# The adaLN modulation of a two-layer streaming encoder, in blocks of 512 features turned by VectorE, sixteen of them between stages

## The reference

```python
c_act = jax.nn.silu(c)
mods = (c_act @ w_ada[l] + b_ada[l]).reshape(bsz, N_SUB, 3, D_MODEL)
shift, scale, gate = mods[:, :, 0], mods[:, :, 1], 1 + mods[:, :, 2]
h = _modulate(x, shift[:, 0], scale[:, 0])            # x * (1 + scale) + shift
f1 = _swiglu(h, ffn_w_gate[l, 0], ffn_w_up[l, 0], ffn_w_down[l, 0])
x = _layer_norm(ALPHA * x + 0.5 * gate[:, 0, None, :] * f1, ln_g[l, 0], ln_b[l, 0])
```

## Time and profile before

| what | value |
|---|---|
| median of 3 runs | 1809.65 us (1809.06 to 1810.31) |
| the profiled execution | 1802.38 us, its span 1800.6 us |
| TensorE (PE) busy | 1669.1 us (93%) |
| VectorE (DVE) busy | 760.9 us (42%) |
| ScalarE (ACT) busy | 648.4 us (36%) |
| GpSimd (POOL) busy | 255.9 us (14%) |
| bytes moved | 301.42 MB, 167 GB/s over the span |
| mean granted TensorE clock | 0.969 |

### The profile page before, as it was taken

One profiled execution on the slowest core, in us unless ns is written; L12 is line 12 of the kernel. 1 busy time (PEld: TensorE's weight loads), 2 busy tenths in 40 slices (PEclk: granted clock), 3 DMA queues, 4 the chain that ended last, 5 costly groups with the idle time before them and its releaser, 6 DMA issues. The chain is left out here.

```text
span 1800.6 us, 30095 instructions
## 1 busy us (share of the span) xinstructions
PE 1669.1 (93%) x11414; PEld 1520.8 (84%) x11414; DVE 760.9 (42%) x1042; ACT 648.4 (36%) x1114; POOL 255.9 (14%) x286
## 2 busy tenths in 40 slices
PE   5999999789977999999789999999889997999996
PEld 3999999678757999989688999989776586999996
DVE  2433333532258433343652433344534465343454
ACT  3433333332244433333342433333334334333332
POOL 1200011220126000011250000011230143000021
PEclk9999999989978999999899999999899998999998
DMA  7544465559813353556335453556353742434441
GB/s 284 211 171 178 160 222 187 201 164 270 253 37 105 142 208 140 198 189 221 120 86 187 168 194 143 206 188 215 112 194 103 271 162 93 141 123 134 129 141 47
DMA packets 88240, 301.42 MB, mean 167 GB/s; under 512 B 11048, under 2 KB 15816, under 8 KB 86736
## 3 DMA queue, kind: packets, MB, share of 16 engines
q1 hardware_dynamic: 83072, 287.62, 46.3%
q10 hardware_dynamic: 5088, 12.69, 2.4%
HBM read 283.58 MB, written 6.00 MB: 161 GB/s over the span
## 5 line engine op out<-in xcount | busy, mean ns | idle before, releaser
L1242 PE MATMUL bank<-hH,wH 128*128 128x384 f32 x1536 | 525.7, 342 | 14.9 <-DVE hL L986 14.1
L623 ACT ACTIVATE wH<-raw 128x1024 fp32r<-128x1024 f32 x328 | 345.1, 1058 | 523.1 <-PE bank L1242 416.7
L903 DVE TENSOR_TENSOR wL<-raw,wH 128x1024 fp32r<-128x1024 f32 x328 | 414.6, 1289 | 251.8 <-ACT wH L623 249.2
L1242 PE MATMUL bank<-hL,wH 128*128 128x384 f32 x1536 | 517.0, 337 | 0.0
L1242 PE MATMUL bank<-hH,wL 128*128 128x384 f32 x1536 | 516.8, 336 | 0.0
L1242 PEld LDWEIGHTS bank<-hH,wH 128*128 128x128 f32 x1536 | 291.0, 189 | 31.3 <-issue 23.4
L1242 PEld LDWEIGHTS bank<-hL,wH 128*128 128x128 f32 x1536 | 291.1, 190 | 0.4
L1242 PEld LDWEIGHTS bank<-hH,wL 128*128 128x128 f32 x1536 | 290.7, 189 | 0.0
L1033 DVE TENSOR_TENSOR tmp<-sg,bank 128x384 f32<-128x384 f32 x88 | 48.7, 554 | 479.1 <-PE bank L1242 451.7
L1242 PE MATMUL bank<-hidH,wH 128*128 128x384 f32 x704 | 241.3, 343 | 0.0
L1242 PE MATMUL bank<-hidL,wH 128*128 128x384 f32 x704 | 235.6, 335 | 0.0
(11 more groups left out here) (169 smaller groups left out, 1628.2 us busy)
## 6 DMA issues: line engine op xcount, KB each, us to landing
raw<-W SPq DMA_DIRECT2D x328, 512.0 KB, 6.0
araw<-ADA SPq DMA_DIRECT2D x130, 512.0 KB, 4.3
land<-ADA SPq DMA_DIRECT2D x16, 512.0 KB, 15.1
KTb<-kt_d SPq DMA_DIRECT2D x8, 1024.0 KB, 6.1
Vb<-v_d SPq DMA_DIRECT2D x8, 1024.0 KB, 5.2
araw<-ADA ACTq DMA_DIRECT2D x14, 512.0 KB, 6.2
u<-uF SPq DMA_DIRECT2D x64, 81.5 KB, 4.9
u<-uF ACTq DMA_DIRECT2D x64, 81.5 KB, 5.2
```

Source lines behind the costliest of these rows:

```text
L623: a.activation(wH[:, slot, :], raw[:, slot, :], ACT.Copy).then_inc(w_hi, 1)
L903: v.tensor_tensor(wL[:, slot, :], raw[:, slot, :], wH[:, slot, :].bitcast(F32), ALU.subtract)\
L1242: op = mm(out, tile_w(w, slot, k), m[:, k0 + k, :], start=start and k == 0 and q == 0, stop=stop and k == nk - 1 and q == 2)
```

## The change

The eight first chunks stay chunks of 256 features with 32 short matmuls each (64 columns). The other 72 become 36 blocks of 512 features. A block is four pieces of 512 KB (`ADA` laid out anew), each two of the eight input feature tiles. TensorE makes a piece with 8 matmuls of 128 columns, and the four column groups now hold other output features instead of other input features, so nothing is left to be added. VectorE turns a block with one transpose of 32 x 32 squares and adds the bias (`modulation`). `ada_tr`, `adaS` and ScalarE's two instructions are gone.

The table `PLACES` gives each piece its tile. By it 16 blocks stand between stages, behind `stats` on TensorE (`gap_block`): 3 after FFN0, 2 after the convolution, 3 after pw2, 3 after FFN1, 3 after FFN2, 2 after O. Their pieces go to tiles that lie over memory free at that time (`gapH` and `gapL` over `hH` and `hL`, `gapD` and `gapE` over the hidden layer). The other 20 use the two halves of `araw` as before: 5 in the gate/up loop of FFN0 and of FFN1, 3 in that of FFN2 (each over two steps, a piece in each half step), 1 and 2 in the down products of FFN0 and FFN1, 1 in the convolution, 3 in the attention, none in FFN3.

Besides, `u4` has three slots, the taps of a tile are loaded behind its shifted rows, the `wf` matmuls stand behind the K stage's `lead`, and VectorE splits four units of K before it waits for them.

```diff
+PLACES = (6 * [RAW4] + [GAP_A, GAP_B, GAP_E] + [RAW4] + [GAP_A, GAP_B] + [GAP_D, GAP_F, GAP_E]
+          + 7 * [RAW4] + [GAP_A, GAP_B, GAP_E] + 3 * [RAW4] + [GAP_A, GAP_B, GAP_E] + 3 * [RAW4] + [GAP_D, GAP_F])
...
-        FFN_ADA = [(8, 11, 8), (35, 11, 8), (54, 11, 8), (77, 3, 0)]
+        FFN_ADA = [(0, 5, 1), (15, 5, 2), (25, 3, 0), (36, 0, 0)]
+        FFN_GAP = [(6, 7, 8), (22, 23, 24), (28, 29, 30), ()]
...
@@ SyncE
-            def ada_chunk(c):
-                sp.wait_ge(a_mm, c)
-                for j in range(2):
-                    sp.dma_start(araw[:, j], ADA[2 * c + j]).then_inc(a_in[j], 16)
+            def loop_piece(s, kq):
+                sp.wait_ge(a_mm, 4 * s + kq + 1)
+                sp.dma_start(araw[:, kq % 2], ADA[4 * s + kq]).then_inc(piece_in[RAW4[kq]], 16)
...
-                with sp.Fori(0, na) as i:
-                    ada_chunk(c + i)
-                    w_units(u + RING + RING * i, RING)
+                if n_up:
+                    with sp.Fori(0, n_up) as i:
+                        for half in range(2):
+                            loop_piece(s + i, 2 * half)
+                            loop_piece(s + i, 2 * half + 1)
+                            w_units(u + RING + 8 * i + 4 * half, RING)
+                with sp.Fori(2 * n_up, 11) as i:
                     w_units(u + RING + RING * i, RING)
...
+                    w_unit(u + 48 + m, m % RING)
+                sp.wait_ge(w_used, u + FFN_UNITS)
+                for kq in range(4):
+                    piece(gap[2], kq)
...
@@ VectorE
+            def modulation(s, bank=ADB):
+                dve.wait_ge(a_mm, 4 * s + 6)
+                dve.wait_ge(a_mod, s + 1)
+                v.transpose(adaT[:].rearrange("p m c -> p (m c)"), bank[:, 0:P]).then_inc(a_tv, 1)
+                dve.wait_ge(a_tv, s + 2)
+                k = 2 * FIRST_CHUNKS + 4 * s
+                v.tensor_tensor(mods[:, bass.ds(k, 4), :], adaT[:, :, 0:NG],
+                                pcol("b_ada", k, 4).unsqueeze(2).to_broadcast([P, 4, NG]), ALU.add).then_inc(a_mod, 1)
...
+            dve.sem_inc(a_mm, 2)
+            dve.sem_inc(a_tv, 1)
+            dve.sem_inc(a_mod, 1)
...
@@ TensorE
+            def four_blocks(out, cols, tile, k, start, stop):
+                for j in range(4):
+                    op = mm(out[32 * j:32 * j + 32, 0:cols], cact[:, k, :], tile[:, cols * j:cols * j + cols],
+                            start=start, stop=stop)
+                return op
+            def ada_piece(kq, tile, bank=ADB):
+                for kk in range(2):
+                    op = four_blocks(bank, P, tile[:, kk], 2 * kq + kk, kq + kk == 0, kq + kk == 4)
                 op.then_inc(a_mm, 1)
...
+            def gap_block(s, place, second=bank[5]):
+                out = second if place == 1 else ADB
+                pe.wait_ge(a_tv, s + 1 if place == 0 else s)
...
-                with pe.Fori(1, na) as i:
-                    gate_up(i, True, c + i - 1)
+                if n_up:
+                    with pe.Fori(0, n_up) as i:
+                        gate_up(2 * i + 1, s + i, 0)
+                        gate_up(2 * i + 2, s + i, 1)
```

More of the change, by code:

```diff
@@ L321, in w_units, with piece @@
                     w_unit(n + j, j % RING, wait)
-            def ada_chunk(c):
-                sp.wait_ge(a_mm, c)
-                for j in range(2):
-                    sp.dma_start(araw[:, j], ADA[2 * c + j]).then_inc(a_in[j], 16)
+            def piece(s, kq):
+                place, before = PLACES[s][kq], PIECE_USES[4 * s + kq][1]
+                if before is not None and place[:3] == "raw":
+                    sp.wait_ge(a_mm, eaten(before))
+                sp.dma_start(piece_tile(place), ADA[4 * s + kq]).then_inc(piece_in[place], 16)
@@ L939, in normalise @@
                 if h:
+                    if gap:
+                        dve.wait_ge(a_mm, last_in("HL", gap) if any(PLACES[s][1][0] in "HL" for s in gap) else 2)
                     rest(*h, 0, 1)
                     rest(*h, 1, 1)
+                if gap:
+                    modulation(gap[0])
+                    modulation(gap[1], second)
                 mean_out(4, 2)
@@ L1149, in _ @@
             modulate(4)
-            for n in range(U_K + RING, U_V + RING):
+            for n in range(U_V, U_V + RING):
                 refill(n, n % RING)
@@ L1204, in body @@
                 for j in range(4):
+                    if kind == "p" and j == 1 and (not isinstance(i, int) or i > 0):
+                        modulation(B_ATT - 1 + i)
                     if scores:
@@ L1307, in stats, with gate_up @@
                 mm(VAR[:, 0:T], ones, sqb[:, 1], start=False, stop=True).then_inc(var_ok, 1)
+                for place, s in enumerate(gap):
+                    gap_block(s, place, second)
             def ffn(fi):
-                u, (c, na, nd) = FFN_U[fi], FFN_ADA[fi]
+                u, (s, n_up, n_down) = FFN_U[fi], FFN_ADA[fi]
                 m = FFN_M[fi]
-                def gate_up(i, with_ada, turn_of=None):
+                def gate_up(i, block=None, half=0):
                     for j in range(2):
@@ L1527, in turn, with body @@
                 nc.tensor.transpose(bank[4 + (j + 1) % 2][:, 384:512], om[:, j % 2, :], ident).then_inc(o_mm, 1)
[L1529 removed]
+            def body(kind, i, block=None, new=True):
                 for j in range(4):
@@ L1539, in body @@
                         turn(*jo)
-                    if with_ada and j == 2:
-                        ada_mm(CH_S4 + i, araw, ring_waits(CH_S4 + i))
-                    if with_ada and j == 3:
-                        ada_tr(CH_S4 + i)
-            body("p", 0, True)
-            with pe.Fori(1, 4) as i:
-                body("p", i, True)
+                    if block is not None:
+                        loop_piece(block, B_ATT, j)
+            body("p", 0, B_ATT)
+            with pe.Fori(1, 3) as i:
+                body("p", i, B_ATT + i)
+            body("p", 3)
             body("s", 0)
```

384 lines of the change are left out of this document (216 added, 168 removed).

## The result

The changed kernel takes **1988.68 us** (median of 4 runs, 1983.57 to 1991.97), the kernel before 1809.36 in the same series: **1.0988** times as long, 95% interval [1.0963, 1.1013]. The forecast was 1981, the range 1925 to 2035. The profiled execution is the one of 1983.57 us, with a span of 1981.8.

The account below looks back on a forecast made before the run. The prediction took TensorE's work plus 131 us without work as the bound. Smaller terms of -60.5 us and a +232 us stall made +171.5, added to 1809.65 for 1981 us; range 1925 to 2035.

Parts of the forecast that it names:

- The deciding term, +232: Gate/up loops of FFN0, FFN1, FFN2: weights requested only after the previous step ends; 23 steps at 10.1 us, +232 us.
- ScalarE waits 5 to 6 us for raw weights: Expected trace sign: ScalarE waits 5 to 6 us for raw weights in each of the 23 stalled steps.
- The 4.4 worked out beside it: Alternative estimate for two loads at a stall: 4.4 us instead of 5.4, making the sum lower by some 23 us.
- The lower bound of the idle part, 6.6: Least idle TensorE time per stalled step, from the fastest weight landing of 3.4 us; 8.3 with the clock, 191 us.
- Loops and down products, -53: FFN loops and down products: 16 blocks costing 48 us replace 60 chunks costing 101 us; -53 us.
- rival (b): VectorE's transpose stands behind late units' splitting and delays the next block's piece 0: 3 us in 13 blocks, 2020 us; 8%.
- Convolution, -22: The convolution loses eight chunks, their load waits and perhaps 4.61 us ahead of the taps, and gains one block; -22 us.
- Start, -5: The start loses the turning and its ScalarE waits in four pairs of chunks; -5 us (0 to -8).
- K, -7: K stage: `lead` no longer behind `wf` matmuls, 12.7 us go, some 5 come back, VectorE may cost 1; -7 us.
- VectorE's chain behind them may cost 1: K stage: VectorE's chain behind the moved `wf` matmuls may cost 1 us.
- Attention, +7: Attention: three blocks replace four chunks (+2), and the first piece's load wait grows by some 5 us; +7 us.
- Gaps, +14, +4, +1.5: Between stages: third blocks in four gaps +14 (0 to 21), loads ahead of `conv_in` +4, turns after the convolution +1.5.

Follow-up runs that it names:

- the kernel with the weights first: The changed kernel with the weight loads issued ahead of the two modulation loads in all three gate/up loops; 1769.35 us, 0.9774 of the kernel before.

## Why the prediction was right, and where its terms missed

**What bounds the kernel.** Right: TensorE, with new idle time as the only way to lose 180 us. ScalarE and VectorE stayed at 30% and 39%.

**The deciding term, +232.** Right in mechanism, place and count: 23 steps, first weight load issued 0.7 us behind the step's end, the low clock behind each stall, 28 us between gate outputs (27.3 to 29.7 in FFN0, a little above the 25 to 28 forecast), 16.64 in FFN3. Its size was a little high: 9.5 us a step where 10.1 was taken, 219 in all. The idle part is 175.3 / 23 = 7.6, not 8.1; the clock's 1.9, not 2.0. The sign "ScalarE waits 5 to 6 us for raw weights" was badly put: from the step's end it does, but the profile counts from its last work and shows 17 to 19. By the idle part the two loads took about 4.9 us where 5.4 was taken from the rows. The 4.4 worked out beside it from the fit in the Trainium skill ("DMA: Bandwidth & Descriptors", Anatomy of one DMA) rests on a figure that the section gives for transfers issued by GpSimd, while SyncE issues these. The lower bound of the idle part, 6.6, holds some 0.5 us between the queue's wake and the first weight load that the text doesn't name; with the terms that it names it is 6.1.

**Loops and down products, -53.** Read from the kernel with the weights first, where no stall hides it: gate and up products -21.9, FFN3 -5.2, down products -26.9. That is -54, but -4.6 of it lies in the three `lead`s and belongs to other terms (-3.7 to the start, -2.0 in FFN1's is clock given back, FFN2's is 1.1 longer). The term itself came out at -49. A half step with a piece takes 9.09 us, that without 8.32: 0.77 a piece, 0.73 was taken. One stretch missed inside the sum: FFN1's down product, with two blocks, gave 3.0 where the prediction's prices make 7.5, and that is the whole miss of this term. The second block waits there for VectorE's transpose of the first, which stands behind the split of a weight that ScalarE had just rounded (TensorE's and VectorE's rows of the changed kernel):

```profile
956.80 0.64 PE L1389 MATMUL bank<-araw,cact 128*32 128x128 f32 x16 [2.63 <-DVE adaT L974]
...
955.29 1.23 DVE L967 TENSOR_TENSOR wL<-raw,wH 128x1024 fp32r<-128x1024 f32 x1 [2.41 <-ACT wH L726]
956.43 0.31 DVE L974 STREAM_TRANSPOSE adaT<-bank 128x128 f32<-128x128 f32 x1
```

That is rival (b), the late turn, at one place of the program where two blocks follow each other closely; the wait is 2.6 us of the 4.5, and in the gate/up loops there is none.

**Convolution, -22.** -21.1, though one part of it failed: the 4.61 us ahead of the taps did not go but became 7.1, a wait for `taps`. So this part came out 7 us worse than said, and the other parts together some 6 us better; 1.3 us of this is pw1's `lead`, which runs at the full clock now (17.9 us for 19.2), the rest wasn't traced.

**Start, -5.** Right in the main: -3.8 us in the changed kernel. Up to FFN0's first unit matmul nothing was gained (-0.1). The loads for the start land at their own time, and TensorE waits for them longer where it has less to do:

```profile
24.94 1.94 PE L1389 MATMUL bank<-land,cact 128*32 128x64 f32 x64 [11.06 <-DMA land<-ADA]
```

6.77 us stood there before. The two pairs inside the `lead` wait for no load, and there the turning was worth 3.7 us.

**K, -7.** The `lead` came earlier as said, but the step "VectorE's chain behind them may cost 1" looked at VectorE and not at SyncE: the wait on `ncum_done` has V's weights behind it. That is 5.7 us of idle time. The stages from FFN1 to V came out at +3.1 together, where -7 and the gap's +3.5 were forecast. The run with V's loads early gives 6.4 us of it back.

**Attention, +7.** +13.8. The wait grew by what was said (4.7 to 11.6 us in three waits), but the price of a wait is more than its length: the stage's mean clock fell from 0.96 to 0.90 and TensorE's busy time in it rose by 5.2 us (107.9 to 113.1). Two waits of 1.0 us for a transpose are new as well. In the loops the prediction counted the clock, here it didn't.

**Gaps, +14, +4, +1.5.** A block behind a transpose, about 5 us in each of four gaps: measured 4.9 ahead of Q and 6.0 ahead of FFN1. The clock given back is the shorter `lead` behind them, 2.7 and 2.5 us, so the net price is 2.2 and 3.5 us where 3.5 was forecast. After FFN0 it is +7.9 with `conv_in`, 6.6 net, against 7.5. The two-block gap after the convolution took 1.2 us; that after O, for which nothing was counted, 2.4. The third block's own price by the run that removes it is 12 to 17 us for four gaps, against 14.

**The sum.** The terms besides the stall made -41 us (1769.35 against 1810.0) instead of -60.5, the stall 219 instead of 232. Most of the 20 us lie in the attention (7), K and V (7) and FFN1's down product (4.5). The misses of 20 and 13 us had opposite signs, so the total was off by 8 us. That it came closer than its parts is luck; that it came out within the range is not, since the stall alone lay well inside its bounds (219 between 191 and 271).

## What to carry to other kernels

On a queue that issues in order, a wait belongs to everything behind it: before a load with a wait is placed ahead of the weights of the next step, compare when its wait is met with when those weights are needed, and put the urgent, unguarded loads first. Where the profile names an engine that only copies or turns as the releaser, look at what stands ahead of that copy on its engine: for `mods` and for `kF` it was a weight that had not landed. Price a stall with the slow clock behind it, a quarter on top of the idle time for the 7.6 us stalls here and over a third for those of 6.0 us, and check the queue of every engine that a moved step's semaphore releases, not only that of the engine that computes it.

## What the runs showed of the hardware

The clock falls and comes back by what TensorE does and not by what the results are for: dummy matmuls into an unread bank in a 7 us gap kept it at 1.00 where it had been at 0.50. A shorter stall isn't cheaper behind it: 6.0 us of idle time cost 2.2 us more at the low clock, 7.6 us cost 1.9. VectorE's transpose of 128x128 fp32 from PSUM takes 303 to 319 ns, in all 36 instances:

```profile
L974 DVE STREAM_TRANSPOSE adaT<-bank x36: 303/309/319, 111.5 to 1688.5; 128x128 f32<-128x128 f32 x36
```

The Trainium skill ("VectorE: DVE Perf Modes", The three transpose paths) gives 311 ns for bf16; for fp32 from PSUM this case's trace shows the same time.
